# Two neighbouring weight rows per partition for the down units of an expert layer

## The reference, cut to what matters

```
def swiglu(x, wg, wu, wd):
    return (jax.nn.silu(x @ wg) * (x @ wu)) @ wd

def moe_swiglu(x, w_router, b_router, wg, wu, wd):
    ...
    for e in range(N_EXPERTS):
        out = out + combine[..., e:e + 1] * swiglu(x, wg[e], wu[e], wd[e])
```

## Time and profile before

| | us |
|---|---|
| median of three runs | 1321.56 |
| the runs | 1319.52, 1324.35, 1321.56 |
| span of the profiled execution | 1319.5 |
| expert stage in it, from the first expert subtractions in close order to the last cast | about 430 to 1291 |
| PE busy | 1267.1 (96%) |
| DVE busy | 1129.3 (86%) |
| ACT busy | 929.9 (70%) |

### The profile page before, as it was taken

How to read it: one execution, slowest core, us unless ns; L and a number is a source line. 1 busy time by engine, 2 the same in 40 slices (tenths; PEclk the granted TensorE clock), 3 DMA queues, 4 the chain that set the end, 5 groups by cost and what they waited for, 6 DMA issues and landing times.

```text
span 1319.5 us, 16344 instructions
## 1 busy us (share of the span) xinstructions
PE 1267.1 (96%) x6161; PEld 1033.9 (78%) x6161; DVE 1129.3 (86%) x944; ACT 929.9 (70%) x747; POOL 92.8 (7%) x111
## 2 busy tenths in 40 slices
PE   7989999999999999999999999999999999999996
PEld 6987888888977778778877777887777787677774
DVE  5887644457988899999998999898999989899997
ACT  5555444435544788888886888887888888788883
POOL 2660000000750000000000000000000000000000
PEclk9999999999999999999999999999999999999998
DMA  9637555544352999999999999999999999999992
GB/s 310 234 127 242 186 189 190 192 160 160 130 172 83 396 394 375 389 399 404 409 409 409 389 411 394 409 409 409 399 388 405 398 409 409 409 390 402 397 406 93
DMA packets 133045, 425.10 MB, mean 322 GB/s; under 512 B 9008, under 2 KB 11344, under 8 KB 132960
## 3 DMA queue, kind: packets, MB, share of 16 engines
q1 hardware_dynamic: 131600, 420.21, 83.7%
q0 software_dynamic: 1216, 3.71, 0.9%
q10 hardware_dynamic: 144, 0.07, 0.0%
HBM read 422.91 MB, written 1.05 MB: 321 GB/s over the span
## 4 chain that ended last, share of the span: by engine, by line
PE 70%; DVE 16%; issue 7%; ACT 4%; SPq 1%; DMA 1%; DVEq 0%; ACTq 0%
PE bank L1783 18%; PE bank L1785 17%; PE bank L1784 17%; DVE w_lo L1182 8%; PE bank L2117 6%; PE bank L2118 5%; DVE arena L1285 1%; DVE w_lo L1204 1%; PE bank L2163 1%; DMA raw<-in_w_in 1%; PE bank L2150 1%; ACT w_hi L841 1%; DVE parts L1655 1%; PE bank L2091 1%; PE bank L2113 1%
## 5 line engine op out<-in xcount | busy, mean ns | idle before, releaser
L1182 DVE TENSOR_TENSOR w_lo<-raw,w_hi 128x2048 fp32r<-128x2048 f32 x216 | 485.9, 2286 | 31.6 <-PE bank L1785 16.0
L821 ACT CAST w_hi<-raw 128x2048 fp32r<-128x2048 f32 x216 | 408.0, 1916 | 62.7 <-PE bank L1785 61.4
L1783 PE MATMUL bank<-w_hi,parts 128*128 128x512 f32 x824 | 328.6, 399 | 13.1 <-DVE w_lo L1182 7.3
L1785 PE MATMUL bank<-w_hi,parts 128*128 128x512 f32 x824 | 321.5, 390 | 0.0
L1784 PE MATMUL bank<-w_lo,parts 128*128 128x512 f32 x824 | 321.0, 390 | 0.0
L2117 PE MATMUL bank<-w_hi,parts 128*128 128x512 f32 x672 | 270.9, 403 | 8.4 <-ACT arena L1048 3.0
L2118 PE MATMUL bank<-w_lo,parts 128*128 128x512 f32 x672 | 263.6, 392 | 0.0
L1783 PEld LDWEIGHTS bank<-w_hi,parts 128*128 128x128 f32 x824 | 154.8, 188 | 55.4 <-issue 21.2
L1204 DVE TENSOR_TENSOR w_lo<-raw,w_hi 128x2048 fp32r<-128x2048 f32 x60 | 138.6, 2311 | 60.8 <-PE bank L1785 46.3
L1182 DVE TENSOR_TENSOR w_lo<-arena,w_hi 128x2048 fp32r<-128x2048 f32 x80 | 181.1, 2286 | 2.3 <-ACT w_hi L821 2.0
L1785 PEld LDWEIGHTS bank<-w_hi,parts 128*128 128x128 f32 x824 | 154.7, 188 | 33.0
(11 more groups left out here) (260 smaller groups left out, 1262.3 us busy)
## 6 DMA issues: line engine op xcount, KB each, us to landing
raw<-in_wu_exp SPq DMA_DIRECT2D x76, 1024.0 KB, 11.3
raw<-in_wg_exp SPq DMA_DIRECT2D x70, 1024.0 KB, 10.3
raw<-in_wd_exp SPq DMA_DIRECT2D x70, 1024.0 KB, 10.7
arena<-in_wd_exp SPq DMA_DIRECT2D x29, 1024.0 KB, 10.4
arena<-in_wg_exp SPq DMA_DIRECT2D x26, 1024.0 KB, 11.0
arena<-in_wu_exp SPq DMA_DIRECT2D x25, 1024.0 KB, 10.7
raw<-in_w_in SPq DMA_DIRECT2D x20, 1024.0 KB, 5.8
tokens<-in_wg_exp SPq DMA_DIRECT2D x16, 1024.0 KB, 11.9
```

The source lines that it names most:

```text
L821: a.copy(to, ring[s]).then_inc(hi_ready, 1)
L1182: v.tensor_tensor(low(n), ring[s], high(n).bitcast(F32), ALU.subtract).then_inc(lo_ready, 1)
L1783: mm(psum, left[0], right[0], start=first, stop=False)
L1785: return mm(psum, left[1], right[0], start=False, stop=last)
```

## The change

A down unit takes 256 neighbouring rows of wd and gives partition p the rows 2p and 2p + 1 of them. They are neighbours in memory, so a partition's part is one run of 8 KB. Source and destination of the DMA become plain two-dimensional (128 x 2048). Row group jj of the unit then holds the even (0) or odd (1) rows, so the transposes take, of the 256 hidden features of a unit, the even or odd columns: `feature_rows` views 256 columns as 128 pairs and picks one of each pair. The number and sizes of DMAs, transposes and matmuls are the same. Gate, up, mixer and dense units are as before.

```
         def expert_source(kind, b, half, e):
-            w = {"g": wg_exp, "u": wu_exp, "d": wd_exp}[kind][0, e].rearrange("(k p) n -> p k n", p=P)
             if kind == "d":
-                k0 = EBLK // P * b + 2 * half
-                return w[:, k0:k0 + 2, :]
+                r0 = EBLK * b + 2 * P * half
+                return wd_exp[0, e][r0:r0 + 2 * P, :].rearrange("(p j) n -> p (j n)", j=2)
+            w = {"g": wg_exp, "u": wu_exp}[kind][0, e].rearrange("(k p) n -> p k n", p=P)
...
             def fetch(s, src, landed_at):
-                n = src.shape[2]
-                sp.dma_start(ring[s].rearrange("p (k n) -> p k n", n=n), src).then_inc(landed_at[0], 16)
+                dst = ring[s]
+                if len(src.shape) == 3:
+                    dst = dst.rearrange("p (k n) -> p k n", n=src.shape[2])
+                sp.dma_start(dst, src).then_inc(landed_at[0], 16)
...
+            def feature_rows(gates, rows, j):
+                c0 = j // 2 * 2 * P
+                return gates[0:rows, c0:c0 + 2 * P].rearrange("p (f r) -> p r f", r=2)[:, j % 2, :]
...
-                        last = tr(bank[WORK_A + half][:, (j % 4) * P:(j % 4 + 1) * P], esg[:, j * P:(j + 1) * P], ident)
+                        last = tr(bank[WORK_A + half][:, (j % 4) * P:(j % 4 + 1) * P], feature_rows(esg, P, j), ident)
...
-                    last = tr(bank[WORK_B][:, j * NARROW:(j + 1) * NARROW], esg_n[0:NARROW, j * P:(j + 1) * P],
+                    last = tr(bank[WORK_B][:, j * NARROW:(j + 1) * NARROW], feature_rows(esg_n, NARROW, j),
                               ident[0:NARROW, 0:NARROW])
```

## The result

The changed kernel is slower: median 1325.97 us over 22 runs (1321.47 to 1328.31), against 1322.19 for the kernel before over 22 runs (1317.10 to 1325.78). The ratio is 1.0030, interval 1.0021 to 1.0038. The forecast was 1320.5, that is no change.

What follows compares the result with a forecast made beforehand. Compute, not loads, was taken to bound the expert stage, at 219.2 us per pair of experts. DMA 0 plus transposes 0 on the 1319.5 us profiled execution, plus 1.0 towards the median, gave 1320.5 us; range 1315 to 1329.

Steps and rivals of the forecast that it cites:

- the price of the transposes: 224 hidden-activation transposes on PE, weight load reading columns 8 bytes apart: taken as 0, bounds 0 to 20.2 us.
- So the loads set its pace: Wide stream of eight transposes: 0.11 us each, less than the weight load's 140 ns record, so weight loads set the pace.
- Looks like the array taking columns: Transposes' weight loads: one column per 0.85 ns read as the array's limit, not memory's, so a stride costs 0.
- its rule of two accesses in 16 bytes: Transposes' strided SBUF reads: full rate while two successive accesses share 16 bytes, so columns 8 bytes apart cost 0.
- Rival 2: Strided weight loads slow in the 224 transposes: 10.8 to 20.2 us more, 1330 to 1340 us; chance 0.14.
- DMA side 0: Down-unit loads: 8.4 us of DMA time spared over 112 units, none of it reaching the end.
- rival 3: Down loads: 8 KB runs cut up again into 4 KB packets, no change, 1319.5 to 1321.6 us; chance 0.10.
- The slack of 3.0 us: Expert stage, per pair of experts: DMA needs 216.2 us against 219.2 us of compute, 3.0 us short of limiting.
- A stage limited by memory would not keep such time: Expert stage: DVE's wait returning every 219.2 us taken as a sign that compute, not loads, sets the pace.
- The last 12 loads reach nobody: End of the expert stage: last 12 loads, all down units, land about 0.9 us earlier with nobody waiting.
- +1.0 us for runs with late loads: Added to the 1319.5 us profiled span: halfway to the 1321.56 us median, whose excess may partly be late loads.
- Nothing hides a slower load: Behind a transpose stream: the next product's first weight load comes before the stream's record ends, so slower loads have no cover.

Runs made afterwards that it cites:

- experiment 7: The kernel before, with the transposes' streamed identity kept in every second column of a second tile and read with step 2; one run, 1322.79 us.
- experiment 1: The kernel before, with only the 224 transposes changed to take every second column, loads as before; ratio 1.0038.
- experiment 6: The kernel before, with all 224 transposes taking every fourth column, loads as before; ratio 1.0031.
- experiment 2: The kernel before, with only the down loads changed to one 8 KB run per partition, old transposes; ratio 1.0011.
- experiment 5: The changed kernel's 8 KB loads, with silu and product separating even and odd features so transposes take neighbouring columns; ratio 0.9999 to the kernel before.
- 9: The kernel before, with wide down products using two matmuls in place of three (less PE work), 4 KB runs; ratio 0.9933, median 1312.65 us.
- 10: 8 KB loads, even and odd features separated in silu and product, wide down products cut to two matmuls; 0.9894 against the kernel before, median 1306.64 us.
- experiment 8: The kernel before, with each down unit loaded as four 2 KB runs per partition, transposes as before; ratio 1.0055.

## Why the prediction was wrong

The step that failed is the price of the transposes: "I take 0: the loads take about one column per 0.85 ns (0.109 us for 128), which looks like the array taking columns rather than memory giving them." Two of its readings were wrong.

- *"So the loads set its pace."* The rows said otherwise. Narrow transposes load the same 128 columns as wide ones and followed each other at 0.063 to 0.07 us, so a load of 128 neighbouring columns takes no more than that. What differed was the streamed identity, 64 columns against 128. So it was the streamed side and not the load that set the wide pace of 0.109 us (experiment 7 shows it move with the identity alone), and the load was hidden behind it. What set the narrow pace of 0.063 us no run shows; it may be the load itself.
- *"Looks like the array taking columns."* With a step the load needs 0.12 us whether 64 or 128 rows are loaded and whether the step is 2 or 4 (experiments 1, 6). With a stream of 128 columns (0.109) nearly all of it stays hidden and 11 ns show; with 64 columns (0.063) half of it shows, about 59 ns. The narrow streams, the smaller work, paid more.

The Trainium skill, "SBUF — State Buffer", section "Door 1: The DMA port swizzle", gave 0 by its rule of two accesses in 16 bytes. The runs do not agree for this load: 8 bytes apart costs as much as 16 bytes apart (209 and 209 ns for the wide loads), and both 69 ns more than neighbours.

Rival 2 was the right mechanism at the wrong size. It had 18 ns for each transpose as the point from which it decides; measured were 59 and 11, on average 35. On PE that is about 7.2 us, from the starts of the transposes (12.3 against 6.8 us for 96 narrow gaps, 11.3 against 10.5 for the wide) and of the product behind each stream; less than its 10.8 to 20.2. Nearly half of it was absorbed where PE would have waited, so 3.9 us came out. It had a chance of 0.14.

The other steps:

- *DMA side 0*: right. Rate 422 GB/s as worked out, 14,336 packets fewer (131,600 to 117,264), which rules out rival 3, and no gain (experiments 2 and 5). The landings came earlier by 0.4 to 0.6 us in the median, not by 1 or 2. The mechanism named, that the compute never waits for loads, is shown by what happens when it is shortened (9, 10) or the loads are lengthened (8). The slack of 3.0 us, an average over the period, was too large: the loads bind in stretches of it (8).
- *"A stage limited by memory would not keep such time."* Wrong as a sign: the kernel of experiment 8, which does wait for its loads, repeated its first 80 units to 0.05 us. That the loads did not bind was right by the waits alone.
- *The last 12 loads reach nobody*: DVE's tail was busy as before; nothing in the runs speaks against it.
- *+1.0 us for runs with late loads*: wrong. The scatter of the runs follows PE's clock, and the kernels with faster loads scatter as much (a standard deviation of 1.9 and 1.7 us in experiments 2 and 5, 1.7 before). With the 1.8 us between a run's span and its time in its place the forecast would have been 1321.3 us, no change.
- *Nothing hides a slower load*: wrong in part; half of the cost on PE met its later waits.

## What to carry to other kernels

When a step goes from contiguous to strided, ask of each engine separately: here the same step of two was free for ACT and DVE on PSUM and about doubled the spacing of PE's transposes where the stream was short. So do the reordering in an elementwise pass that exists anyway, and give PE neighbouring columns. Before pricing an operation by its cadence, look for a second row where one of its two sides is shorter: it bounds what the other side needs, and so how much cover there is. And a supply that is fast enough on average can still bind in a stretch of slower loads that is longer than the ring.

Faster transfers pay only where the compute waits for them. Whether they will is better read from who waits, and from a run with the compute shortened, than from a busy share near 1.

## What the runs showed of the hardware

- Fp32 transposes whose weight load has 128 columns follow each other at as little as 0.063 us with neighbouring columns, at 0.12 us with every second or every fourth, for 64 and for 128 rows. The streamed operand took 0.109 us for 128 neighbouring columns and 0.116 us with step 2.
- Runs of 2, 4 and 8 KB from main memory moved 387, 410 and 422 GB/s: by these, as an estimate, 75 ns for each 2 KB and a fixed cost of about 10 ns a run.
- In the 57 runs of the kernel before about three quarters of the variance in time go with PE's mean granted clock, 1.0 us for each 0.001. One stretch of 3.4 us at half clock, with PE busy throughout, cost 1.6 us (15.2 against 13.6 us for the last four units of a period). The length of a repeating period within one trace (219.12 and 219.18 us) resolved 0.3 us in 219, where medians of 12 runs resolved 1 to 2 us in 1320.
